# Summing a token's two expert rows with a 128-row product and two column tiles

## The chip, the cores and the metric

The kernel runs on one core of a Trainium2 chip. The metric is the device time of one execution in microseconds; lower is better. A core has TensorE (matrix products, into PSUM), VectorE, ScalarE and GpSimd (elementwise work), SyncE (SP, which here issues most transfers), and 16 transfer engines that all queues share.

## The reference, cut to what matters

One inference step of a small decoder with two layers, for 1024 prompt tokens and 8 sample tokens of 1024 float32 features. Each layer mixes (sliding-window attention and a short gated convolution), normalises, and then runs a mixture of 32 experts, of which each token uses two:

```python
x = layer_norm(ALPHA * x + mixer(x), ln1_g, ln1_b)
x = layer_norm(ALPHA * x + hier_moe(x), ln2_g, ln2_b)   # hier_moe: y[token] = sum over its 2 experts of gate * mlp_e(x[token])
```

The change is in how the two expert results of a token are added and handed to that last layer norm.

## The kernel before, in words

**Data.** Tokens lie in nine tiles: tiles 0 to 7 have 128 tokens (NB = 8), tile 8 (t == NB) has the 8 sample tokens. T is 1032. The DRAM tensor `ytok` has the shape (2, T, 1024): for each token and each of its two experts (k = 0, 1) one row of 4 KB, written by indirect transfers of the experts' results (the residual is already in them). `rows_of` is the same tensor seen as 2T rows, so row t*128 + i holds token i of tile t for k = 0, and row T + t*128 + i holds it for k = 1.

**The seam and the tail.** After the 32 experts of a layer, SP waits for all indirect writes and then loads the rows (L515 to L532). `first_in(t)` brings the k = 0 rows of tile t into `xin[t]`, and `second_in(t)` the k = 1 rows into `second[t]`. A transfer has 128 partitions and 512 KB; both count up the semaphore `l2_in{t}`. In the last layer this is done for all nine tiles. In the first layer it is done for tiles 0 to 4 (SUMMED = 5); tiles 5 to 8 only get their first row from SP, in between, and GpSimd later adds the second row to it with an accumulating transfer (`second_added`, L2067 to L2072). GpSimd issues that after its part of the norm of tile t - 5 and after waiting for `l2_in{t}`.

**The sum on TensorE.** `outputs_summed(l, t)` (L556 to L571) waits for both rows of a tile, and for a free pair of PSUM banks (a ring of two pairs in the first layer, of four in the last). For each half of the 1024 features it makes two products with the identity as weights, which accumulate in one bank: the first rows, then the second rows (L567, L569). A float32 product appears as two instructions in the trace. In the first layer tiles 0 and 1 are summed at the end of the layer (L1077); the sums of tiles 2, 3 and 4 stand in the next layer's program, each ahead of `x_turned(t)`, the transposes of tiles 0, 1 and 2 (L599 to L602). Then the projections of the next layer begin (`first_project`, L595) with the turns of tiles 3 to 8 between them.

**The norm.** VectorE takes statistics of the sum in PSUM (`statistics2`, L1862), GpSimd the inverse root (`inverse2`), VectorE subtracts the mean and multiplies by the gain into `xin[t]` (`shifted2`, L1881), then multiplies by the inverse root and adds the bias (`scaled2`, L1887), and counts up `x2_ready`. In the first layer the order is shifted(p-1), statistics(p), scaled(p-1). In the last layer ScalarE takes the statistics of tiles 1 to 8 (L1286, L1298). SP stores each finished tile from `xin[t]` (L536), after all the loads in its queue. The next layer's transposes read `xin[t]`.

**A load elsewhere.** At the start of each layer SP loads the output weights `wo` in three transfers, with rows of 4 KB: two of 1 MB into partitions 0 to 63 and 64 to 127, then one of 2 MB into all partitions:

```python
                for h in range(NKV):
                    sp.dma_start(wo[h * HD:(h + 1) * HD, 0:4],
                                 a["w_o"][l, h * QPK * HD:(h + 1) * QPK * HD].rearrange("(k p) n -> p k n", p=HD)
                                 ).then_inc(s["wo_in"], 16)
                sp.dma_start(wo[:, 4:8], a["w_o"][l, NH * HD:].rearrange("(k p) n -> p k n", p=P)).then_inc(s["wo_in"], 16)
```

**Column tiles elsewhere.** The down projection of an expert with at most 64 tokens uses two column tiles of TensorE, one product into PSUM partitions 0 to 63 (L969) and one into 64 to 127 (L971).

Of the kernel before, what the change touches and what calls it, by code (L numbers as in the profile page):

```python
# [11 lines left out]
ALU = mybir.AluOpType  # L12
# [3 lines left out]
P = 128  # L16
DM = 1024
KD = DM // P
DEPTH = 2
SEQ = 1024  # L20
NS = 8
T = SEQ + NS
NB = SEQ // P
# [19 lines left out]
HALF = P // 2  # L43
# [10 lines left out]
BASE = 2  # L54
# [3 lines left out]
SUMMED = 5  # L58


def rows_in(l, t):

    return 16 + (32 if t < SUMMED else 16) * l


def settle(eng, passed):


    eng.sem_inc(passed, 1)
# [35 lines left out]
def build(nc, a):  # L105

    ctx = ExitStack()
    with ctx:
        def sb(name, shape, dt=F32):
            return ctx.enter_context(nc.sbuf_tensor(name, shape, dt))  # L110
# [7 lines left out]
        rows_of = a["ytok"].rearrange("k t d -> (k t) d")  # L118


        ident = sb("ident", [P, P])
        ones = sb("ones", [P, P])
        upper = sb("upper", [P, P])
        iota = sb("iota", [P, P])
        masks = sb("masks", [P, 3, 2 * P])
# [46 lines left out]
        def at(off, *shape, parts=P):  # L172
            n = int(np.prod(shape))
            v = arena[0:parts, off:off + n]
            if len(shape) == 2:
                return v.rearrange("p (a b) -> p a b", a=shape[0])
            if len(shape) == 4:
                return v.rearrange("p (a b c d) -> p a b c d", a=shape[0], b=shape[1], c=shape[2])
            if len(shape) == 3:
                return v.rearrange("p (a b c) -> p a b c", a=shape[0], b=shape[1])  # L180
            return v
# [23 lines left out]
        def ws(off, *shape, parts=P):  # L205
# [59 lines left out]

        passed_over = at(0, 2, DM)
        xin = [at(29552 + 1024 * t, DM) for t in range(NB)] + [at(27496, DM, parts=NS)]
        second = [at(14448 + 1024 * t, DM) for t in range(4)] + [at(o, DM) for o in (37744, 38768, 39792, 28528)] \
            + [at(26464, DM, parts=NS)]
        FIRST3 = [(c, ch) for ch in range(NCH) for c in range(3)]  # L270
        ROTATED = FIRST3 + [(c, ch) for c in (3, 4) for ch in range(NCH)]
        TURNED_WITH = {(1, 0): 3, (2, 0): 4, (0, 1): 5, (1, 1): 6, (2, 1): 7, (0, 2): 8}
# [1 line left out]
        ps = ctx.enter_context(nc.psum_tensor("ps", [P, 8, 512], F32))  # L274
# [52 lines left out]
        def _(sp):  # L327
# [13 lines left out]
            def tile_rows(t):  # L341
                return P if t < NB else NS
# [22 lines left out]
            for l in range(DEPTH):  # L365
# [149 lines left out]
                def first_in(t):  # L515
                    sp.dma_start(xin[t][0:tile_rows(t)], rows_of[t * P:t * P + tile_rows(t), :]
                                 ).then_inc(s[f"l2_in{t}"], 16)

                def second_in(t):
                    sp.dma_start(second[t][0:tile_rows(t)], rows_of[T + t * P:T + t * P + tile_rows(t), :]  # L520
                                 ).then_inc(s[f"l2_in{t}"], 16)

                if l < DEPTH - 1:
                    for t in range(SUMMED):
                        first_in(t)
                        second_in(t)
                        if 0 < t < SUMMED:
                            first_in(SUMMED + t - 1)
                else:
                    for t in range(NT):  # L530
                        first_in(t)
                        second_in(t)  # L532
                for t in range(NT):
                    sp.wait_ge(s["x2_ready"], BASE + NT * (l + 1) + t + 1)
                    settle(sp, s["sp_passed"])
# [8 lines left out]
        def _(pe):  # L544
            raise_to_base(pe, "tensor")
            mm = nc.tensor.matmul
# [9 lines left out]

            def outputs_summed(l, t):

                rows = P if t < NB else NS
                ring = 4 if l == DEPTH - 1 else 2  # L560
                pe.wait_ge(s[f"l2_in{t}"], BASE + rows_in(l, t) + 32)
                if t >= ring:
                    pe.wait_ge(s["l2_used"], BASE + NT * l + t - ring + 1)
                settle(pe, s["pe_passed"])
                for h in range(2):
                    cols = slice(h * 512, (h + 1) * 512)
                    mm(ps[0:rows, 2 * (t % ring) + h, :], ident[0:rows, 0:rows], xin[t][0:rows, cols],  # L567
                       start=True, stop=False)
                    last = mm(ps[0:rows, 2 * (t % ring) + h, :], ident[0:rows, 0:rows], second[t][0:rows, cols],  # L569
                              start=False, stop=True)  # L570
                last.then_inc(s["l2_mm"], 1)  # L571

            for l in range(DEPTH):
# [465 lines left out]
                with pe.If(pe.value_load(over[0:1, OVER:OVER + 1], min_val=0, max_val=OVER) > 0):  # L1039
                    pe.wait_ge(s["ov_m"], BASE + l + 1)  # L1040
                    settle(pe, s["pe_passed"])
                    for i in range(2 * NT):
                        last = mm(ps[:, 0, 0:2 * OVER], over_slot[:, i], over_block[:, i].rearrange("p q n -> p (q n)"),
                                  start=(i == 0), stop=(i == 2 * NT - 1))
# [5 lines left out]
                    with pe.Fori(0, OVER) as o:  # L1050
                        n = OVER * l + o
                        pe.wait_ge(s["ov_xin"], BASE + n + 1)
                        for k in range(KD):
                            last = tr(ps[:, k // 4, (k % 4) * P:(k % 4 + 1) * P], xg_by_row[0][:, k], ident[:])
# [3 lines left out]
                        for f in range(FD):  # L1058
                            for w, bank in ((wg, 2), (wu, 4)):
                                for k in range(KD):  # L1060
                                    last = mm(ps[:, bank, f * P:(f + 1) * P], w[2].rearrange("p k (c f) -> p k f c", f=FD)[:, k, f],
                                              xgT[:, 0, k], start=(k == 0), stop=(k == KD - 1))
                        last.then_inc(s["ov_gu"], 1)
                        pe.wait_ge(s["ov_h"], BASE + n + 1)
                        for h in range(2):
                            for f in range(FD):
                                last = mm(ps[:, 6 + h, :], hT[:, f], wd[0][:, f, h * 512:(h + 1) * 512],
                                          start=(f == 0), stop=(f == FD - 1))
# [244 lines left out]
        def _(dve):  # L1313
            raise_to_base(dve, "vector")
            v = nc.vector
            step = Steps(dve, s["dve_step"])
# [12 lines left out]
            for k in range(2):  # L1329
                step.mark(v.tensor_scalar(token[:, k, 1:NT], tokens1[:, 0:NB], float(k * T - 1 - NONE), None, ALU.add))  # L1330
                step.mark(v.tensor_scalar(token[:, k, 0:1], tokens1[:, NB:NT], float(k * T - 1 - NONE), None, ALU.add))
            step.mark(v.tensor_scalar(bias_row[:], rank_desc[:], NE - FIRST + 0.5, 1e6, ALU.is_gt, ALU.mult))
            for h in range(2):
                step.mark(v.tensor_tensor(perm[:, h * NE:(h + 1) * NE], ident[0:64, h * NE:(h + 1) * NE],
# [20 lines left out]
            for l in range(DEPTH):  # L1355

                for i, (r, ch) in enumerate(ROTATED):
                    cols = slice(ch * CH, (ch + 1) * CH)
                    dve.wait_ge(s["act_ev"], BASE + l * NTILE * NCH + i + 1 + 6)
                    for q in range(4):  # L1360
                        to, of = slice(32 * q, 32 * q + 32), slice(32 * (q ^ 1), 32 * (q ^ 1) + 32)
                        last = v.scalar_tensor_tensor(rot[to, i % 2], ztmp[of, r % 3, cols], 2.0 * (q % 2) - 1,  # L1362
                                                      sinT[of, cols], ALU.mult, ALU.mult)
# [489 lines left out]
                def on_tensor(t):  # L1853
                    return l == DEPTH - 1 or t < SUMMED
# [7 lines left out]
                def statistics2(t, r, p):  # L1862
                    if on_tensor(t):
                        dve.wait_ge(s["l2_mm"], BASE + SUMMED * l + t + 1)
                    else:
                        dve.wait_ge(s[f"l2_both{t}"], 16 * (l + 1))
                    dve.wait_ge(s["l2_stat"], BASE + NT * l + p)
                    for h in range(2):
                        step.mark(v.bn_stats(stat[r, 6 * h:6 * h + 6], summed(t, r)[:, h * 512:(h + 1) * 512]))
                    step.wait()  # L1870
                    settle(dve, s["dve_passed"])
                    v.bn_aggr(mv[r, p % 2], stat[r]).then_inc(s["l2_stat"], 1)

                def shifted2(t, r, p):
                    if l < DEPTH - 1 or p == 0:
                        dve.wait_ge(s["l2_stat"], BASE + NT * l + p + 1)
                        shift, by = mv[r, p % 2, 0:1], ALU.subtract
                    else:
                        dve.wait_ge(s["l2_square"], BASE + p)
                        shift, by = sums[r, p % 4, 1:2], ALU.add  # L1880
                    v.scalar_tensor_tensor(xin[t][r], summed(t, r), shift, lnp[r, 2], by, ALU.mult  # L1881
                                           ).then_inc(s["l2_used"], 1)

                def scaled2(t, r, p):
                    dve.wait_ge(s["l2_used"], BASE + NT * l + p + 1)
                    dve.wait_ge(s["l2_rstd"], BASE + NT * l + p + 1)
                    v.scalar_tensor_tensor(xin[t][r], xin[t][r], rstd[r, p % 2, 0:1], lnp[r, 3], ALU.mult, ALU.add  # L1887
                                           ).then_inc(s["x2_ready"], 1)

                rows_at = [slice(0, P if t < NB else NS) for t in range(NT)]  # L1890
                statistics2(0, rows_at[0], 0)
                if l < DEPTH - 1:
                    for p in range(1, NT):
                        shifted2(p - 1, rows_at[p - 1], p - 1)
                        statistics2(p, rows_at[p], p)
                        scaled2(p - 1, rows_at[p - 1], p - 1)
                    shifted2(NT - 1, rows_at[NT - 1], NT - 1)
                    scaled2(NT - 1, rows_at[NT - 1], NT - 1)
                else:
                    shifted2(0, rows_at[0], 0)  # L1900
                    for p in range(1, NT):
                        shifted2(p, rows_at[p], p)
                        scaled2(p - 1, rows_at[p - 1], p - 1)
                    scaled2(NT - 1, rows_at[NT - 1], NT - 1)
# [264 lines left out]
```

## Time and profile before

| | |
|---|---|
| time, median of 3 runs | 2174.56 us (2174.32 to 2181.47) |
| the profiled execution's own time | 2183.16 us |
| its span | 2181.3 us |
| TensorE matmul busy | 2072.5 us, 95% of the span |
| VectorE, ScalarE, GpSimd busy | 805.1, 325.7, 222.1 us |
| mean granted TensorE clock | 0.974 of full speed |
| transfers | 535.92 MB, mean 246 GB/s |

Times in views of the trace are microseconds from the span's start; those of the two stretches of interest are about 1056 to 1085 (the seam between the layers) and 2129 to 2181 (the tail). A row of the chain of waits gives the start and the length of one link. A row of the timeline gives the start, the length, the engine, the line and the operation; PE is TensorE's products, SPq are issues on SP's queue.

### The profile page before, as it was taken

The page shows a single profiled execution, that of the slowest core. Times are in us where ns is not written, and L with a number is a line of the kernel's source. Part 1 is how long each engine was busy: PE and PEld are TensorE (multiplying, and loading weights), DVE is VectorE, ACT ScalarE, POOL GpSimd, SP SyncE. Part 2 cuts the span into 40 slices and gives each one's busy share as a digit, 9 for nine tenths or more (in the row PEclk, how much of TensorE's full clock was granted, in tenths as well). Part 3 has the DMA queues.
Part 4 walks back from the last instruction along what each step waited for, and adds up shares of the span by engine and source line. Part 5 has one row for each costly group of instructions (what it writes and reads, how often), then busy time and mean ns, then how long its engine had stood idle before and what let it go on. Part 6 is the DMA issues. An engine that isn't in the chain of part 4 may idle for free.

```text
span 2181.3 us, 32300 instructions
## 1 busy us (share of the span) xinstructions
PE 2072.5 (95%) x13024; PEld 1221.7 (56%) x13024; DVE 805.1 (37%) x1547; ACT 325.7 (15%) x856; POOL 222.1 (10%) x250
## 2 busy tenths in 40 slices
PE   8999999989999999899799999999999999999986
PEld 5666655565555655455366666555645556554542
DVE  4512166672222222222482123766622221222224
ACT  2011123311111011111010111333001110110103
POOL 1200000000111111110231000000001100111101
PEclk9999999999999999999899999999999999999997
DMA  6601131348999999998634101413689999999956
GB/s 223 193 30 38 41 128 68 113 158 316 360 392 400 414 384 396 392 387 334 231 123 120 39 29 32 158 59 116 228 325 391 399 406 395 392 388 394 379 219 236
DMA packets 77465, 535.92 MB, mean 246 GB/s; under 512 B 14586, under 2 KB 23674, under 8 KB 52386
## 3 DMA queue, kind: packets, MB, share of 16 engines
q1 hardware_dynamic: 64050, 498.37, 59.5%
q0 software_dynamic: 13264, 35.44, 4.8%
q8 instruction: 107, 1.75, 0.3%
q14 instruction: 44, 0.36, 0.0%
HBM read 494.14 MB, written 54.08 MB: 251 GB/s over the span
## 4 chain that ended last, share of the span: by engine, by line
PE 91%; DVE 4%; issue 3%; DMA 1%; ACT 1%; POOL 1%; DVEq 0%; SPq 0%; POOLq 0%
PE ps L925 20%; PE ps L616 19%; PE ps L969 10%; PE ps L763 9%; PE ps L905 6%; PE ps L595 4%; PE ps L893 3%; PE ps L976 3%; PE ps L921 3%; PE ps L949 2%; PE ps L567 1%; PE ps L963 1%; PE ps L569 1%; PE ps L805 1%; PE ps L705 1%
## 5 line engine op out<-in xcount | busy, mean ns | idle before, releaser
L927 PE MATMUL ps<-arena 128*64 128x256 f32 x1920 | 450.9, 391 | 0.0
L925 PE MATMUL ps<-arena 128*64 128x256 f32 x1920 | 450.9, 391 | 0.0
L616 PE MATMUL ps<-arena 128*128 128x344 f32 x1440 | 421.2, 453 | 0.0
L925 PEld LDWEIGHTS ps<-arena 128*64 128x64 f32 x1920 | 255.0, 135 | 175.9 <-issue 23.9
L616 PEld LDWEIGHTS ps<-arena 128*128 128x128 f32 x1440 | 272.0, 190 | 142.9 <-issue 3.6
L969 PE MATMUL ps<-arena 128*64 128x512 f32 x480 | 236.5, 639 | 22.3 <-issue 19.9
L927 PEld LDWEIGHTS ps<-arena 128*64 128x64 f32 x1920 | 254.5, 135 | 0.0
L971 PE MATMUL ps<-arena 128*64 128x512 f32 x480 | 236.8, 640 | 0.0
L763 PE MATMUL ps<-arena 128*128 128x512 f32 x448 | 195.9, 594 | 2.7 <-issue 2.7
L1703 DVE SCALAR_TENSOR_TENSOR arena<-ps,gates,arena 64x256 f32<-64x256 f32 (+1 forms) x128 | 60.9, 476 | 354.9 <-ACT arena L1228 354.9
L1970 POOL DMA_INDIRECT ytok<-arena,gidx x64 | 60.3, 942 | 955.3 <-DVE arena L1731 924.2
L763 PEld LDWEIGHTS ps<-arena 128*128 128x128 f32 x448 | 84.0, 190 | 105.1 <-issue 105.1
L969 PEld LDWEIGHTS ps<-arena 128*64 128x64 f32 x480 | 65.1, 145 | 137.0 <-issue 133.8
L1228 ACT ACTIVATE arena<-ps 64x256 f32<-64x256 f32 (+1 forms) x128 | 48.9, 382 | 618.9 <-PE ps L927 535.7
L905 PE MATMUL ps<-arena 128*32 128x256 f32 x2048 | 129.4, 405 | 10.7 <-DVE arena L1724 9.2
L905 PEld LDWEIGHTS ps<-arena 128*32 128x32 f32 x2048 | 68.2, 112 | 77.4 <-issue 36.2
L1093 ACT COPY arena<-ps 128x344 f32<-128x344 f32 x90 | 40.1, 446 | 361.1 <-PE ps L616 324.1
L1944 POOL TENSOR_SCALAR rstd<-mv 128x1 f32<-128x1 f32 (+1 forms) x18 | 21.6, 1203 | 693.8 <-DVE mv L1353 693.8
L595 PE MATMUL ps<-arena 128*128 128x344 f32 x288 | 86.0, 454 | 5.6 <-ACT arena L1100 5.6
L1362 DVE SCALAR_TENSOR_TENSOR arena<-arena,sinT 32x344 f32<-32x344 f32 x120 | 76.6, 638 | 26.2 <-ACT arena L1093 16.5
L1119 ACT ACTIVATE arena<-arena,sm 128x256 f32<-128x256 f32 x128 | 63.7, 499 | 90.5 <-DVEq L1438 90.5
L595 PEld LDWEIGHTS ps<-arena 128*128 128x128 f32 x288 | 53.6, 190 | 32.3 <-issue 6.5
(262 smaller groups left out, 2133.0 us busy)
## 6 DMA issues: line engine op xcount, KB each, us to landing
arena<-in_w_gate SPq DMA_DIRECT2D x64, 2048.0 KB, 24.0
arena<-in_w_up SPq DMA_DIRECT2D x64, 2048.0 KB
arena<-in_w_down SPq DMA_DIRECT2D x64, 2048.0 KB
arena<-in_w_in SPq DMA_DIRECT2D x36, 512.0 KB, 3.5
ytok<-arena SPq DMA_DIRECT2D x32, 512.0 KB, 3.5
arena<-ytok SPq DMA_DIRECT2D x29, 512.0 KB, 9.3
arena<-out_y_all SPq DMA_DIRECT2D x16, 512.0 KB, 3.5
out_y_all<-arena SPq DMA_DIRECT2D x16, 512.0 KB
```

The lines of the kernel that those rows point to most:

```text
L595: last = mm(ps[:, bank, 0:CH], wring[:, c, k * P:(k + 1) * P], xT[:, k, ch * CH:(ch + 1) * CH], start=(k == 0), stop=(k == KD - 1))
L616: last = mm(ps[:, 3 * half + ch, 0:CH], wring[:, slot, k * P:(k + 1) * P], xT[:, k, ch * CH:(ch + 1) * CH], start=(k == 0), stop=(k == KD ...
L763: last = mm(ps[0:rows, 6 + n, :], mix[k], wo[:, k, n * 512:(n + 1) * 512], start=(k == 0), stop=(k == KD - 1))
L893: last = tr(ps[:, k // 4, (k % 4) * P:(k % 4) * P + rows], xg_by_row[slot + 2 * (turn % 2)][0:rows, k], ident[0:rows, 0:rows])
L905: last = mm(ps[QUART * t:QUART * (t + 1), 5, 0:256], xgT[:, slot, k, HALF:MID], w[slot3][q][:, k], start=(k == 0), stop=(k == KD - 1))
L921: last = mm(ps[:, 2 + q, at_c:at_c + 256], xgT[:, slot, k], w[slot3][q][:, k], start=(k == 0), stop=(k == KD - 1))
L925: mm(ps[HALF:P, 2 + q, 0:256], xgT[:, slot, k, 0:HALF], wg_half[slot3][q][:, k], start=(k == 0), stop=(k == KD - 1))
L927: last = mm(ps[0:HALF, 2 + q, 0:256], xgT[:, slot, k, 0:HALF], wu_half[slot3][q][:, k], start=(k == 0), stop=(k == KD - 1))
L969: mm(ps[0:HALF, 6, :], hT[:, f, 0:HALF], wd[slot][:, f, 0:512], start=(f == 0), stop=(f == FD - 1))
L971: last = mm(ps[HALF:P, 7, :], hT[:, f, 0:HALF], wd[slot][:, f, 512:DM], start=(f == 0), stop=(f == FD - 1))
L976: last = mm(ps[QUART * t:QUART * (t + 1), 5, 0:256], hT[:, f, HALF:MID], wd[slot][:, f, t * 256:(t + 1) * 256], start=(f == 0), stop=(f == ...
L1362: last = v.scalar_tensor_tensor(rot[to, i % 2], ztmp[of, r % 3, cols], 2.0 * (q % 2) - 1, sinT[of, cols], ALU.mult, ALU.mult)
```

## The change

The two rows of a token are put on partitions i and 64 + i of one tile: `xin[t]` gets both rows of the first 64 tokens of tile t, `second[t]` both rows of the other 64. `both` is a 128 x 64 matrix of two identities, so one product with it as weights adds the two rows of 64 tokens. Its result goes to PSUM partitions 0 to 63 for `xin[t]` and 64 to 127 for `second[t]`, which are two column tiles of TensorE. Each tile is loaded by four transfers of 64 partitions and 256 KB in place of two of 128 partitions and 512 KB. The 8-row tile gets 16 partitions, `both_s`, and its own weights, `both8`. VectorE builds both matrices at the start. In the first layer, VectorE now scales tile 0 before it takes the statistics of tile 1. The tiles that GpSimd adds (5 to 8 in the first layer) stay as they were.

```diff
 def rows_in(l, t):
-    return 16 + (32 if t < SUMMED else 16) * l
+    return 16 + (64 if t < SUMMED else 16) * l
...
+        both = sb("both", [P, HALF])
+        both8 = sb("both8", [2 * NS, NS])
...
-        second = [at(14448 + 1024 * t, DM) for t in range(4)] + [at(o, DM) for o in (37744, 38768, 39792, 28528)] \
-            + [at(26464, DM, parts=NS)]
+        second = [at(14448 + 1024 * t, DM) for t in range(4)] + [at(o, DM) for o in (37744, 38768, 39792, 28528)]
+        both_s = at(27496, DM, parts=2 * NS)
...
-                def second_in(t):
-                    sp.dma_start(second[t][0:tile_rows(t)], rows_of[T + t * P:T + t * P + tile_rows(t), :]
-                                 ).then_inc(s[f"l2_in{t}"], 16)
+                def both_in(t):
+                    if t == NB:
+                        for k in range(2):
+                            sp.dma_start(both_s[k * NS:(k + 1) * NS], a["ytok"][k, SEQ:T, :]
+                                         ).then_inc(s[f"l2_in{t}"], 16)
+                        return
+                    for tile, r0 in ((xin[t], t * P), (second[t], t * P + HALF)):
+                        for k in range(2):
+                            sp.dma_start(tile[k * HALF:(k + 1) * HALF], a["ytok"][k, r0:r0 + HALF, :]
+                                         ).then_inc(s[f"l2_in{t}"], 16)
 
                 if l < DEPTH - 1:
                     for t in range(SUMMED):
-                        first_in(t)
-                        second_in(t)
+                        both_in(t)
                         if 0 < t < SUMMED:
                             first_in(SUMMED + t - 1)
                 else:
                     for t in range(NT):
-                        first_in(t)
-                        second_in(t)
+                        both_in(t)
...
             def outputs_summed(l, t):
-                rows = P if t < NB else NS
                 ring = 4 if l == DEPTH - 1 else 2
-                pe.wait_ge(s[f"l2_in{t}"], BASE + rows_in(l, t) + 32)
+                pe.wait_ge(s[f"l2_in{t}"], BASE + rows_in(l, t) + (64 if t < NB else 32))
...
                 for h in range(2):
-                    cols = slice(h * 512, (h + 1) * 512)
-                    mm(ps[0:rows, 2 * (t % ring) + h, :], ident[0:rows, 0:rows], xin[t][0:rows, cols],
-                       start=True, stop=False)
-                    last = mm(ps[0:rows, 2 * (t % ring) + h, :], ident[0:rows, 0:rows], second[t][0:rows, cols],
-                              start=False, stop=True)
+                    bank, cols = 2 * (t % ring) + h, slice(h * 512, (h + 1) * 512)
+                    if t == NB:
+                        last = mm(ps[0:NS, bank, :], both8[:], both_s[:, cols], start=True, stop=True)
+                    else:
+                        mm(ps[0:HALF, bank, :], both[:], xin[t][:, cols], start=True, stop=True)
+                        last = mm(ps[HALF:P, bank, :], both[:], second[t][:, cols], start=True, stop=True)
                 last.then_inc(s["l2_mm"], 1)
...
+            step.mark(v.tensor_tensor(both[:], ident[:, 0:HALF], ident[:, HALF:P], ALU.add))
+            step.mark(v.tensor_tensor(both8[:], ident[0:2 * NS, 0:NS], ident[0:2 * NS, NS:2 * NS], ALU.add))
...
                     for p in range(1, NT):
                         shifted2(p - 1, rows_at[p - 1], p - 1)
+                        if p == 1:
+                            scaled2(0, rows_at[0], 0)
                         statistics2(p, rows_at[p], p)
-                        scaled2(p - 1, rows_at[p - 1], p - 1)
+                        if p > 1:
+                            scaled2(p - 1, rows_at[p - 1], p - 1)
```

## Rows read from the trace of the kernel before

**Rows 1.** The page: busy time and share of each engine.
```profile
PE 2072.5 (95%) x13024; PEld 1221.7 (56%) x13024; DVE 805.1 (37%) x1547; ACT 325.7 (15%) x856; POOL 222.1 (10%) x250
```

**Rows 2.** The chain of waits over the seam: start, length, link.
```profile
1056.37 4.57 DMA arena<-ytok
...
1063.12 1.71 PE ps L569 x2
...
1083.20 0.89 PE ps L583 x8
...
1085.27 4.87 PE ps L595 x16
```

**Rows 3.** The chain of waits over the tail.
```profile
2129.57 4.43 DMA arena<-ytok
2134.14 2.04 PE ps L567 x2
...
2163.22 0.86 PE ps L569 x2
...
2166.74 0.87 PE ps L569 x2
```

**Rows 4.** Timeline of the last expert of each layer: products in column tiles.
```profile
1045.54 1.06 PE L969 MATMUL ps<-arena 128*64 128x512 f32 x1
...
1045.57 1.06 PE L971 MATMUL ps<-arena 128*64 128x512 f32 x1
...
1046.39 1.06 PE L969 MATMUL ps<-arena 128*64 128x512 f32 x1
...
2122.08 0.59 PE L969 MATMUL ps<-arena 128*64 128x512 f32 x1
...
2122.51 0.59 PE L969 MATMUL ps<-arena 128*64 128x512 f32 x1
```

**Rows 5.** Timeline of the seam: issues on SP's and GpSimd's queues.
```profile
1056.37 0.43 SPq L520 DMA_DIRECT2D arena<-ytok  x1
1056.84 0.43 SPq L516 DMA_DIRECT2D arena<-ytok  x1
...
1070.52 1.02 POOL L2071 DMA_DIRECT2D arena<-ytok  x1
```

**Rows 6.** Windows of seam and tail; last columns: granted clock, transfer engines' share, GB/s.
```profile
1059.00:1073.00 14.00, 11.92 (x21) 5.18 (x22) 4.55 (x8) 0.00 (x0) 1.90 (x4) 0.72 1.03 411
...
1065.00:1067.00 2.00, 2.00 (x3) 0.67 (x2) 0.00 (x0) 0.00 (x0) 0.00 (x0) 0.54 1.04 422
...
1075.00:1085.00 10.00, 9.07 (x36) 4.84 (x34) 9.30 (x15) 2.91 (x3) 5.71 (x7) 1.00 1.04 260
...
2132.00:2150.00 18.00, 15.86 (x32) 7.03 (x33) 3.60 (x5) 3.63 (x8) 1.25 (x4) 0.82 1.02 408
```

**Rows 7.** Windows of the `wo` load in both layers; same columns.
```profile
77.00:79.00 2.00, 2.00 (x9) 1.31 (x8) 1.97 (x3) 0.00 (x0) 1.23 (x1) 1.00 1.02 201
79.00:81.00 2.00, 2.00 (x9) 1.31 (x8) 1.15 (x3) 0.00 (x0) 0.00 (x0) 1.00 1.04 223
...
75.00:85.00 10.00, 10.00 (x36) 6.53 (x36) 6.88 (x12) 0.89 (x2) 2.47 (x2) 1.00 1.02 206
...
1148.00:1158.00 10.00, 10.00 (x36) 6.55 (x35) 6.52 (x11) 1.34 (x3) 2.60 (x3) 1.00 1.02 204
87.00:91.00 4.00, 4.00 (x15) 2.64 (x14) 2.56 (x5) 0.45 (x1) 0.61 (x2) 1.00 1.01 401
```

**Rows 8.** Timeline of the tail: ScalarE's and VectorE's work on one tile.
```profile
2160.68 1.03 ACT L1286 ACTIVATE arena<-ps 128x1024 f32<-128x1024 f32 x1 [1.13 <-PE ps L569]
...
2161.69 1.11 ACT L1298 ACTIVATE arena<-ps,sums 128x1024 f32<-128x1024 f32 x1
...
2162.93 1.28 DVE L1881 SCALAR_TENSOR_TENSOR arena<-ps,sums,lnp 128x1024 f32<-128x1024 f32 x1 [0.96 <-ACT arena L1298]
...
2164.12 1.28 DVE L1887 SCALAR_TENSOR_TENSOR arena<-arena,rstd,lnp 128x1024 f32<-128x1024 f32 x1
```

## The prediction

> **What bounds the kernel now.** I read the busy shares first. TensorE holds 95% of the span [rows 1], so a change counts where TensorE stands still or where it does the changed work itself. The change touches two short stretches only: the seam between the two layers and the tail of the second layer. So I next read the chain of waits over each of them. At the seam it goes through the load of a tile's two rows, then the sums of tiles 0 to 4 on TensorE with the transposes of the next layer between them, then a copy on ScalarE, and the first projection begins at 1085.27 [rows 2]. In the tail it goes through the same load, then 36 products in one unbroken row until 2167.6 (2166.74 and 0.87 more) [rows 3]; ScalarE, VectorE and the last store follow, 13.7 us up to the end of the span at 2181.3. At both places a load ends first and TensorE then sets the pace, so two prices decide: how fast the rows arrive, and how long a tile's sum holds TensorE.
>
> **TensorE's part.** Before, a tile takes four products, each of two instructions (the chain's rows "x2"), with the full 128-column weights. Two instructions take 1.71 us just after a wait, at the low clock (1.2 GHz) [rows 2], and 0.86 us at the high one (2.4 GHz) [rows 3]. That is 6.8 or 3.43 us for a tile. After, a tile takes four products with 64-column weights, two and two in different column tiles. The down projection does this already: an instruction of L969 and one of L971 start 0.03 us apart, and the next L969 starts 0.86 us later at the low clock and 0.43 us later at the high one [rows 4]. A pair thus costs what one full-width instruction costs, and a tile's sum falls to 3.43 us (low) or 1.71 us (high). The last tile, of 8 rows, goes from four products to two that stand alone: 1.71 us at the high clock, 3.43 at the low one. If nothing else changed, this would take 1.71 us from each of eight tiles of the tail.
>
> **The loads' part.** The bytes stay the same (1.05 MB for a tile), but each transfer is 64 partitions wide instead of 128. Five tiles at the seam go from 10 transfers to 20, eight tiles of the tail from 16 to 32. Issuing one costs SP about 0.45 us (two starts are 0.47 apart [rows 5]), so the first tile's last transfer is issued 0.9 us later; after that issuing, 1.8 us for a tile, is faster than either rate below. The question is the rate. With 128 partitions the loads run at 411 GB/s at the seam and at 408 in the tail, with the transfer engines' share at 1.0 [rows 6]: 2.56 us for a tile. The trace has one load of the new kind: w_o goes into partitions 0-63 and 64-127 in two transfers of 1 MB, one right after the other, from rows of 4 KB. It moves 206 GB/s in layer 0 and 204 in layer 1, with the engines' share again at 1.0, and the following transfer into all 128 partitions is back at 401 [rows 7]. Two queued transfers to opposite halves did not make up for each other. At 205 GB/s a tile takes 5.1 us. The new transfers change halves every 256 KB and not once per MB. The 2 us in which w_o changes halves show 223 GB/s beside 201 before it [rows 7], about 0.04 MB or 0.2 us gained at a hand-over; four in each tile would bring 5.1 down to 4.3 us, and none leaves 5.1. As in layer 1 windows vary as much with no hand-over in them, I lean to the upper end and take 4.9 us.
>
> The Trainium skill, SBUF — State Buffer, section "Can I just issue two DMAs to hit both halves?", says no: a 64-partition transfer reaches half of the memory's ports, and two concurrent ones, at partition 0 and at 64, were only 6% faster than one. The w_o rows agree. By its 6% a tile would take 4.8 us in place of 5.1.
>
> **The seam.** Before, tile 0's rows are there at 1060.94 (1056.37 and 4.57) and the last of the five sums ends at 1083.2, where the turn of tile 2 begins [rows 2]. After, in the order of the queue, with 4.9 us for a tile and 1.28 us for each first row of tiles 5 to 7 that lies between: tile 0 at 1063.3 (2.34 later than at 2.56 us), tile 1 at 1068.2, then tiles 2, 3 and 4 each 1.28 and 4.9 later. The adding transfers of GpSimd fall among them. The first was issued at 1070.52 [rows 5]; its three full ones and the first stores leave 260 GB/s in the ten microseconds from 1075 [rows 6], in which 2.6 MB would take 6.3 us at 411: 3.7 us lost, 1.2 for each of three, and 1.3 for its own half megabyte. Before they ran behind the loads. Now each can run before one of the loads of tiles 2 to 4, as it waits for a first row that lies one tile ahead of them: 2.5 us each. Tile 4 is then there at 1068.2 + 3 x (1.28 + 2.5 + 4.9) = 1094.3. Its sum takes 1.7 or 3.4 us, since TensorE stands idle for a few microseconds before each tile; I take the middle, 2.6. It ends at 1096.9, 13.7 us later than before. The turn and copy behind it keep their length. The clock came back about 5 us after the first product: at the seam it is still 0.54 between 1065 and 1067, and the mean of 0.82 over the 18 us from 2132 means 6.5 us at 0.5, up to 2138.5 [rows 6]; a projection that starts low would lose half of that, 2.5 us, and I count 1.2. The seam costs +14.9 us (ends: +2.4 with 4.3 us, no collision and the high clock; +17 to +21 with 5.1 us, dearer adding transfers and the low clock). The projections behind it are TensorE's own work, so this isn't won back.
>
> VectorE scales tile 0 one step earlier, ahead of tile 1's statistics. This frees tile 0 some 2 us sooner, but its turn on TensorE stands behind the sum of tile 2, which now waits for rows: nothing. If rows came at the old rate it would be worth up to 1 us. Its two small operations that build the summing weights lie in the first layer's preparation, a few tenths of a microsecond on an engine that is 37% busy [rows 1]: nothing, and 0.3 us without that cover. Nothing new waits on GpSimd's or SP's queue but what the later rows delay: the stores of the finished tiles lie behind all loads, as before.
>
> **The tail.** Before, tile 0's rows are there at 2134.0 [rows 3]. After, at 2136.3, and tile 7's 7 x 4.9 later, at 2170.6. From then TensorE has that tile and the 8-row one to do, 2.6 us each by the same middle: 2175.8, against 2167.6 before. +8.2 us (ends: +1.9 with 4.3 us and the high clock, +12 with 5.1 and the low one). The stores have about 2.6 MB to catch up once the loads are out, 6.4 us at 408 GB/s, which ends inside the 13.7 us that follow.
>
> **Sum.** 14.9 + 8.2 = 23.1 us. The profiled execution took 2183.2 us (span 2181.3), 8.6 above the median of 2174.56; the sum made against it gives 2206.3, and on the median 2197.7. I say 2197.5.
>
> **The rivals.** (1) The loads keep their rate, because small transfers to the two halves run side by side. For it: w_o has only one change of halves in a layer, so no row shows an alternating load. Against it: 204 to 206 GB/s with both transfers in the queue. Then the tail is paced by the loads (2.56 us a tile), by ScalarE (1.03 and 1.11 us and their read-outs) and VectorE (1.28 and 1.28) [rows 8], all about 2.6 us in place of TensorE's 3.43. The first sum ends at 2134.9 + 3.4, and the 8-row tile's near 2159.2, 8.4 us earlier; the seam gives 2.3 us by the first sum and some 0.7 by the shorter later ones. -11.4 us: 2163. It decides if a tile arrives in under about 3.2 us. (2) They overlap in part, 300 GB/s, 3.5 us a tile: the tail's pace is then the old 3.43 and its end is set by two short sums, -4 us; the seam gains on VectorE's side and loses by the collisions, +2 to +6. About 2174, no change. (3) The column tiles don't overlap and a sum keeps 3.43 us: rows 4 speak against it, and under a 4.9 us load it would add under 4 us; it stands inside the upper end.
>
> **How the numbers follow.** Half rate, as reckoned: 0.74; its own range is 2179 (+4 by the lower ends) to 2208. Full rate 0.14, partly overlapped 0.12. The predicted time is that of the first. The range is 2170 to 2208: it takes in the second rival and leaves out the first (0.14) and what lies above the upper ends (0.05). A measurement here tells about 0.5%, 11 us, from no change. Slower by more: 0.70 of the first case and 0.02 of the partial one, 0.72. Within: 0.04 of the first, 0.10 of the partial, 0.06 of full rate, 0.20. Faster: 0.08.
>
> **What would show it.** In the windows of the changed kernel's loads: 205 to 240 GB/s with a share of 1.0, where 408 to 411 stood; if it is 400, the forecast falls. TensorE waiting on the load before each tile, not only before tile 0. Pairs of sum instructions 0.43 or 0.86 us apart. The first projection 13 to 16 us later after tile 0's load is issued than now; if only some 7, the adding transfers didn't collide. The last sum 6 to 12 us later in the tail. The prediction is wrong if a tile takes under 4 us to arrive.

## The result, and the profile after

The changed kernel takes 2198.17 us (median of 7 runs, 2194.13 to 2209.7) against 2179.57 of the kernel before on the same chips (2174.32 to 2189.01). The ratio is 1.009, 95% interval [1.0071, 1.011]: slower by 0.9%. The medians differ by 18.6 us and the ratio makes 20 us (15 to 24 by its interval). The forecast was 2197.5 us and slower.

The page after, the same row as [rows 1]:

```profile
span 2207.8 us, 32320 instructions
...
PE 2065.4 (94%) x13020; PEld 1213.1 (55%) x13020; DVE 804.9 (36%) x1549; ACT 324.9 (15%) x856; POOL 221.5 (10%) x250
```

TensorE has 7 us less to do and the span is 26.5 us longer. The windows of the changed kernel, same columns as [rows 6], the first three at the seam and the last three in the tail:

```profile
1063.00:1065.00 2.00, 0.00 (x0) 0.00 (x0) 0.00 (x0) 0.00 (x0) 0.00 (x0) 0.50 0.99 231
...
1091.00:1093.00 2.00, 0.68 (x4) 0.40 (x6) 1.13 (x1) 0.00 (x0) 0.89 (x3) 1.00 0.99 381
...
1097.00:1099.00 2.00, 0.89 (x3) 0.68 (x4) 2.00 (x2) 0.97 (x1) 1.62 (x2) 1.00 0.32 107
...
2153.00:2183.00 30.00, 19.12 (x48) 4.61 (x48) 10.22 (x10) 8.94 (x19) 3.03 (x8) 0.63 1.03 229
...
2187.00:2189.00 2.00, 1.16 (x6) 0.54 (x8) 1.49 (x2) 0.56 (x3) 0.74 (x2) 0.94 1.03 418
2189.00:2191.00 2.00, 2.00 (x5) 0.10 (x2) 0.98 (x1) 0.32 (x1) 0.00 (x0) 0.50 1.03 420
```

For thirty microseconds of the tail the transfer engines are as fully occupied as before (share 1.03) and move 229 GB/s where [rows 6] have 408. From 2187 on, when the last row has come and the stores of 128 partitions run, the rate is 418 to 420. The timeline of TensorE shows what this does. First the seam, tiles 0 to 4, then the first projection:

```profile
1065.82 1.08 PE L576 MATMUL ps<-arena,both 128*64 128x512 f32 x1 [13.07 <-DMA arena<-ytok]
...
1070.44 0.61 PE L576 MATMUL ps<-arena,both 128*64 128x512 f32 x1 [1.02 <-DMA arena<-ytok]
...
1076.40 1.09 PE L576 MATMUL ps<-arena,both 128*64 128x512 f32 x1 [4.02 <-DMA arena<-ytok]
...
1084.39 1.09 PE L576 MATMUL ps<-arena,both 128*64 128x512 f32 x1 [3.54 <-DMA arena<-ytok]
...
1092.32 0.61 PE L576 MATMUL ps<-arena,both 128*64 128x512 f32 x1 [2.43 <-DMA arena<-ytok]
...
1098.11 4.87 PE L602 MATMUL ps<-arena 128*128 128x344 f32 x16 [1.19 <-ACT arena L1107]
```

TensorE now waits for the load before each tile, where before it waited once. The steps are 4.6 and 6.0 us, then 8.0 and 7.9. In the tail the eight tiles come 4.6 us apart; the first, the last, and the 8-row tile:

```profile
2155.48 1.09 PE L576 MATMUL ps<-arena,both 128*64 128x512 f32 x1 [12.95 <-DMA arena<-ytok]
...
2187.84 0.64 PE L576 MATMUL ps<-arena,both 128*64 128x512 f32 x1 [2.62 <-DMA arena<-ytok]
...
2190.57 3.58 PE L574 MATMUL ps<-arena,both 16*8 16x512 f32 x4
```

To compare kernels I take two lengths from each trace. The seam is from the issue of its first load to the start of the first projection; the tail is from the issue of its first load to the end of the last sum. Before, they are 29.3 us (1055.99 to 1085.27) and 38.4 us (2129.18 to 2167.6). After, they are 39.8 us (1058.33 to 1098.11) and 46.0 us (2148.18 to 2194.15). That is +10.5 and +7.6, in all +18.1 us, beside the 18.6 us between the medians. The other 8 us of the profiled executions' difference lie outside them, 2.3 ahead of the seam and 6.2 from the projection to the tail, where the change touches nothing. The latter stretch is 1043.9 us long before, 1050.1 after, and between 1039.1 and 1048.0 in the eight experiments below, without relation to what they change. The two lengths vary too where nothing on their path was changed, by 1 to 1.5 us: e7 has a seam 1.0 us shorter than before and a tail 1.5 us longer. A difference of one microsecond between two of these lengths shows nothing by itself.

### The profile page after: what moved, and what is told of

Same layout as the page of the kernel before. It is cut to its first block, busy times and chain, and to the rows that moved or that the text cites. A ratio compares the mean times of both kernels' runs of the same rounds, so it can differ in the third digit from the quotient of the medians.

```text
span 2207.8 us, 32320 instructions
## 1 busy us (share of the span) xinstructions
PE 2065.4 (94%) x13020; PEld 1213.1 (55%) x13020; DVE 804.9 (36%) x1549; ACT 324.9 (15%) x856; POOL 221.5 (10%) x250
## 4 chain that ended last, share of the span: by engine, by line
PE 88%; DVE 4%; issue 3%; DMA 2%; SPq 1%; ACT 1%; POOL 1%; DVEq 0%; POOLq 0%
PE ps L932 20%; PE ps L623 19%; PE ps L976 10%; PE ps L770 9%; PE ps L912 6%; PE ps L602 4%; PE ps L900 3%; PE ps L983 3%; PE ps L928 3%; DMA arena<-ytok 2%; PE ps L956 2%; SPq L529 1%; PE ps L970 1%; PE ps L812 1%; PE ps L712 1%
## 5 line engine op out<-in xcount | busy, mean ns | idle before, releaser
L623 PEld LDWEIGHTS ps<-arena 128*128 128x128 f32 x1440 | 272.0, 190 | 142.9 <-issue 3.6
L770 PEld LDWEIGHTS ps<-arena 128*128 128x128 f32 x448 | 84.0, 190 | 105.1 <-issue 105.1
L1371 DVE SCALAR_TENSOR_TENSOR arena<-arena,sinT 32x344 f32<-32x344 f32 x120 | 74.9, 624 | 26.2 <-ACT arena L1100 16.5
L576 PE MATMUL ps<-arena,both 128*64 128x512 f32 x52 | 39.0, 894 | 48.3 <-DMA arena<-ytok 48.3
```

Source lines behind the costliest of these rows:

```text
L623: last = mm(ps[:, 3 * half + ch, 0:CH], wring[:, slot, k * P:(k + 1) * P], xT[:, k, ch * CH:(ch + 1) * CH], start=(k == 0), stop=(k == KD ...
L770: last = mm(ps[0:rows, 6 + n, :], mix[k], wo[:, k, n * 512:(n + 1) * 512], start=(k == 0), stop=(k == KD - 1))
```

## The experiments

The theory (H) is that of the prediction: a load into one half of the partitions runs at a little over half the rate, and the two halves do not make up for each other in a queue. The rivals: the loss comes from the number and size of the transfers (S), from the column tiles, or from the source that jumps between the two sets of rows.

**e1_half_loads**, the loads' part alone, on the kernel before:

```diff
...
+                def both_in(t):
+                    if t == NB:
+                        first_in(t)
+                        second_in(t)
+                        return
+                    for tile, r0 in ((xin[t], t * P), (second[t], T + t * P)):
+                        for h in range(2):
+                            sp.dma_start(tile[h * HALF:(h + 1) * HALF], rows_of[r0 + h * HALF:r0 + (h + 1) * HALF, :]
+                                         ).then_inc(s[f"l2_in{t}"], 16)
...
```

> The loads' part of the change alone: the kernel before, with every 128-partition row load of tiles on TensorE split into two of 64 partitions; sums with the identity as before. If loads into one half of the partitions are slow (theory H), the tail's tiles arrive 4.6 us apart as in the changed kernel, the sums hide under them but for the last two, and the kernel is as slow as the changed one or some 3 us slower: +18 to +24 us. If the loss came from the column tiles or their weights (rival), this kernel runs as before, within 3 us.

Measured: ratio 1.0102 [1.0083, 1.0121], 22 us slower. The window of its tail:

```profile
2153.00:2180.00 27.00, 23.86 (x48) 9.41 (x47) 10.22 (x10) 8.98 (x19) 3.02 (x8) 0.91 1.04 229
```

The rate is that of the changed kernel, 229 GB/s, with sums of full width and a source that does not jump. The seam takes 41.9 us and the tail 46.9: +12.6 and +8.4. The changed sums and the source are thus not what costs the time; beside this kernel, the changed one is 3 us shorter in the two stretches.

**e2_pairs**, the same sums, with a token's two rows on partitions 2i and 2i+1:

```diff
...
-                        for k in range(2):
-                            sp.dma_start(tile[k * HALF:(k + 1) * HALF], a["ytok"][k, r0:r0 + HALF, :]
-                                         ).then_inc(s[f"l2_in{t}"], 16)
+                        sp.dma_start(tile, a["ytok"][:, r0:r0 + HALF, :].rearrange("k t d -> t k d")
+                                     ).then_inc(s[f"l2_in{t}"], 16)
...
-            step.mark(v.tensor_tensor(both[:], ident[:, 0:HALF], ident[:, HALF:P], ALU.add))
+            step.mark(v.tensor_tensor(both[:], ident[:].rearrange("p (m k) -> p k m", k=2)[:, 0],
+                                      ident[:].rearrange("p (m k) -> p k m", k=2)[:, 1], ALU.add))
...
```

> The same sums in column tiles, but the two rows of a token lie on partitions 2i and 2i+1, so that 64 tokens come in one 128-partition transfer of 512 KB; the summing weights are paired accordingly. If only the reach of a transfer over the partitions matters (H), loads run near 400 GB/s, tiles 2.6 us apart, and the time is about 11 us under the kernel before (ratio 0.995). If a source that jumps between the two row sets is itself slow (rival), windows show 230 GB/s and the time is that of the changed kernel, +18 us.

Measured: 2172.74 us, ratio 0.997 [0.9958, 0.9983], faster by 0.3%, some 6.5 us and not 11. Its window over the tail's loads, and two tiles in a row of its timeline:

```profile
2133.00:2153.00 20.00, 15.14 (x56) 4.36 (x56) 10.10 (x10) 10.25 (x22) 3.02 (x8) 0.84 1.01 397
```

```profile
2148.99 0.61 PE L574 MATMUL ps<-arena,both 128*64 128x512 f32 x1 [0.62 <-DMA arena<-ytok]
...
2151.55 0.61 PE L574 MATMUL ps<-arena,both 128*64 128x512 f32 x1 [0.62 <-DMA arena<-ytok]
```

397 GB/s and 2.56 us a tile, so a source that jumps between the two sets of rows isn't slow. The tail takes 28.6 us, 9.8 less than before. The seam takes 32.3 us, 3.0 more than before, where I expected some 3 less. Its own wait says why:

```profile
1080.27 1.08 PE L574 MATMUL ps<-arena,both 128*64 128x512 f32 x1 [5.84 <-DMA arena<-ytok]
```

This is tile 4, 20.6 us after tile 0 (1059.66). Four tiles at 2.56 us and three first rows at 1.28 make 14.1, and before the change its rows came 14.5 us after those of tile 0. As tile 0 is normalised sooner, GpSimd issues its first adding transfer 12.0 us after the first load's issue (1066.24), where it was 14.5 before [rows 5], and two more about 4 us apart (1070.38, 1074.08). The issue times and the view's times from issue to landing put the landings of the first two at 1075.3 and 1079.2, ahead of tile 4's rows (1080.1); before the change tile 4's rows had landed (1075.4) ahead of the first (1078.3). So the faster sums start transfers that then hold up the load on the path; e6 tests it.

**e3_grouped**, the changed kernel with the order lower, lower, upper, upper:

```diff
-                    for tile, r0 in ((xin[t], t * P), (second[t], t * P + HALF)):
-                        for k in range(2):
+                    for k in range(2):
+                        for tile, r0 in ((xin[t], t * P), (second[t], t * P + HALF)):
```

> The changed kernel with the four transfers of a tile in the order lower, lower, upper, upper half in place of lower, upper, lower, upper: half as many changes of half. By the hand-over theory (the engines that finish early go on in the other half, 0.2 us gained at each change) the tail's rate falls from 229 GB/s to about 217 and tiles arrive 4.85 us apart, +4 us in the two stretches. If the rate has nothing to do with the changes of half, it stays at 229 GB/s and 4.57 us.

Measured: ratio 1.0092 [1.0068, 1.0116], which cannot be told from the changed kernel. The window of its tail:

```profile
2150.00:2182.00 32.00, 19.49 (x54) 5.11 (x56) 12.70 (x12) 10.53 (x23) 3.76 (x10) 0.71 1.04 217
```

217 GB/s and a mean of 4.87 us a tile, as the hand-over theory wanted: with halves changing every 1 MB 205, every 512 KB 217, every 256 KB 229. The 4 us did not come. The slower loads lengthen the seam by 1.5 us, but the tail is 0.6 us shorter, as the clock happened to be high at its last two sums: its 8-row tile takes 1.88 us where the changed kernel's row above has 3.58.

**e4_mid64**, tail loads of the same number and size into partitions 32 to 95; two of each four go to unused places, so the last layer's sums are of stale data:

```diff
...
+                    for t in range(NB):
+                        for k, tile in enumerate((xin[t], free[2 * t], second[t], free[2 * t + 1])):
+                            r0 = t * P + HALF * (k // 2)
+                            sp.dma_start(tile[QUART:P - QUART], a["ytok"][k % 2, r0:r0 + HALF, :]
+                                         ).then_inc(s[f"l2_in{t}"], 16)
...
```

> The changed kernel whose tail loads go, in the same number and size (four of 64 partitions and 256 KB for a tile), into partitions 32 to 95, which lie across both halves; two of four go to unused places, so the last layer's sums are of stale data and its outputs are not the reference's. If the half matters (H), the tail's windows show about 400 GB/s and tiles arrive 2.6 to 2.8 us apart. If the number of transfers or their size matters (rival S: 32 issues of 0.64 us, 256 KB each), the rate stays near 229 GB/s and 4.57 us.

```profile
2137.00:2153.00 16.00, 13.68 (x48) 4.28 (x48) 7.31 (x8) 7.78 (x16) 2.28 (x6) 0.79 1.01 393
```

393 GB/s, 2.56 us a tile, a tail of 29.3 us. Number and size are the same, only the place differs: S falls. (One execution, read for its windows alone.)

**e5_firsts_last**, the changed kernel with the first rows of tiles 5 to 8 behind all rows of tiles 0 to 4:

```diff
                         both_in(t)
-                        if 0 < t < SUMMED:
-                            first_in(SUMMED + t - 1)
+                    for t in range(SUMMED, NT):
+                        first_in(t)
```

> The changed kernel, but at the seam the first rows of tiles 5 to 8 are loaded after all rows of tiles 0 to 4, so no adding transfer of GpSimd can run among them. If the collisions cost what the changed kernel's trace suggests (tiles 3 and 4 arrive 8.0 us after the one before, of which 4.6 are their own, 1.3 the first row between and 2.1 an adding transfer), all tiles arrive 4.6 us apart, tile 4 about 8 us earlier, and the seam from the first load's issue to the first projection shrinks from 39.8 to 32 us or a little more. If the adding transfers run in gaps (rival), only the moved first rows count, 3.8 us.

Measured: ratio 1.0086 [1.0057, 1.0115]; the seam takes 37.4 us and not 32. Tiles 1 and 2 come 4.6 us apart and TensorE waits for no later load, so the collisions are gone. The landings say what they cost. The following are the last two issues for tile 4 and their time to landing, of which the maximum is that of the last, first in this kernel, then in the changed one:

```profile
L529 SPq DMA_DIRECT2D arena<-ytok x2: 597/597/597, 1065.9 to 1066.6; - x2
...
DMA to landing us min/median/max: 12.6/12.9/13.1
```

```profile
L529 SPq DMA_DIRECT2D arena<-ytok x2: 596/596/597, 1071.2 to 1071.8; - x2
...
DMA to landing us min/median/max: 20.0/20.2/20.4
```

Tile 4's rows land at 1079.6 here, 18.4 us after those of tile 0 (1061.3), and at 1092.2 in the changed kernel, 26.5 us after tile 0's (1065.7). The difference is 8.1 us, as the expectation had it. The three first rows account for 3.8 of it (3 x 1.28); the other 4.3 us are adding transfers, and the rival (3.8 us in all) falls.

The seam did not gain these 8 us, as another wait has come in their place. Two rows of its timeline:

```profile
1081.49 1.02 POOL L2083 DMA_DIRECT2D arena<-ytok  x1 [13.68 <-DMA arena<-ytok]
...
1083.66 1.28 DVE L1896 SCALAR_TENSOR_TENSOR arena<-arena,rstd,lnp 128x1024 f32<-128x1024 f32 x1 [8.44 <-POOL rstd L2077]
```

GpSimd does its work here in the order of the program. It waits 13.68 us for the first row of tile 5, and the inverse root of tile 1, for which VectorE waits 8.44 us, stands behind that wait. Neither my theory nor the rival had this.

**e6_pairs_late**, the pairs kernel with the first rows of tiles 5 to 7 one tile later:

```diff
...
                         both_in(t)
-                        if 0 < t < SUMMED:
-                            first_in(SUMMED + t - 1)
+                        if t > 1:
+                            first_in(SUMMED + t - 2)
+                    first_in(NT - 1)
```

> The kernel with pairs on partitions 2i and 2i+1, and the first rows of tiles 5 to 7 each one tile later in SP's queue. There tile 4 came only 20.6 us after tile 0, held up by first rows and adding transfers, and the seam took 32.3 us against 29.3 before the change. With fewer of them ahead, tile 4 should come by some 16 us after tile 0 and the seam take 27 to 29 us; the tail stays at 28.6 us from the first issue to the last sum. Expected 3 to 5 us under the pairs kernel, ratio 0.995. If VectorE or the sample tile sets the seam's end instead, it stays at 0.997.

Measured: 2167.85 us, ratio 0.9945 [0.9928, 0.9962], some 12 us faster than the kernel before; it is the best version found. Against the pairs kernel it gains some 5 us, but the two intervals just overlap. Tile 4 and the first projection:

```profile
1076.60 1.08 PE L575 MATMUL ps<-arena,both 128*64 128x512 f32 x1 [1.74 <-DMA arena<-ytok]
...
1082.13 4.87 PE L601 MATMUL ps<-arena 128*128 128x344 f32 x16 [1.19 <-ACT arena L1106]
```

Tile 4 comes 16.5 us after tile 0 and no longer 20.6, with one first row fewer (1.3 us) ahead of it. The first adding transfer is issued 13.3 us after the first load (1068.32) and lands at 1077.6, after tile 4's rows (1076.5), where in the pairs kernel two had landed before them. This bears out the reading of e2. The seam takes 27.1 us and the tail 28.5: -2.1 and -9.9 us.

**e7_order_only**, VectorE's new order alone on the kernel before (the last part of the change's diff).

> The kernel before with VectorE's new order alone (tile 0 scaled ahead of tile 1's statistics). Theory: nothing, within 1 us, as the turn of tile 0 stands behind the sum of tile 2 on TensorE. Rival: a turn that comes earlier brings the projections up to 2 us forward.

Measured: ratio 0.9999 [0.9983, 1.0015]: nothing, as expected. The seam takes 28.3 us, 1.0 less than before, but the new order is not the reason. The first product of tile 0, that of tile 1 and the turn of tile 0, first before the change, then here:

```profile
1061.08 2.05 PE L567 MATMUL ps<-arena,ident 128*128 128x512 f32 x2 [10.66 <-DMA arena<-ytok]
...
1067.45 1.02 PE L567 MATMUL ps<-arena,ident 128*128 128x512 f32 x2
...
1074.32 1.04 PE L583 MATMUL ps<-ident,arena 128*128 128x128 f32 x8
```

```profile
1059.80 2.05 PE L567 MATMUL ps<-arena,ident 128*128 128x512 f32 x2 [10.59 <-DMA arena<-ytok]
...
1065.42 1.02 PE L567 MATMUL ps<-arena,ident 128*128 128x512 f32 x2
...
1072.29 1.04 PE L583 MATMUL ps<-ident,arena 128*128 128x128 f32 x8
```

In both the turn follows the sum of tile 2 with no wait, 6.87 us after tile 1's first product. The time is gained ahead of that, in the sum of tile 0 (5.6 us in place of 6.4), because the granted clock rose sooner: it is 0.74 from 3.2 to 5.2 us after the first product (1063 to 1065), where before the change it is 0.54 from 3.9 to 5.9 us [rows 6]. VectorE had not begun by then, so the new order can't be the cause. The rival, up to 2 us, falls too.

**e8_two_queues**, the changed kernel's tail loads, lower halves from SP's queue, upper halves from ScalarE's:

```diff
...
+                    for t in range(NB):
+                        for tile, r0 in ((xin[t], t * P), (second[t], t * P + HALF)):
+                            nc.scalar.dma_start(tile[HALF:P], a["ytok"][1, r0:r0 + HALF, :]
+                                                ).then_inc(s[f"l2_in{t}"], 16)
```

> The changed kernel whose tail loads are issued from two queues: the lower halves from SP, the upper halves from ScalarE's queue at the same time, same transfers otherwise. If an engine takes both queues in turn and the halves really are separate resources, both are filled at once and tiles arrive 2.6 us apart (about 400 GB/s). If the engines stay in step, each writing to one half at a time, the rate stays between 205 and 240 GB/s and tiles 4.4 to 5.1 us apart.

Two of its windows:

```profile
2138.00:2140.00 2.00, 0.00 (x0) 0.00 (x0) 0.00 (x0) 0.00 (x0) 0.00 (x0) 0.50 1.04 227
...
2150.00:2152.00 2.00, 1.89 (x8) 0.49 (x8) 0.00 (x0) 0.49 (x4) 0.00 (x0) 1.00 1.03 322
```

It was run once (2185.7 us). It starts at 227 GB/s and settles at 322, 3.24 us a tile, and the tail takes 34.6 us. Both expectations missed: two queues fill the halves better than one, but not fully. Why it takes 6 us to get there stays open.

## Why the prediction was right

**The rate of the loads** was the step that decided, and it held; e1 shows that it alone makes the loss, e4 that the place of the 64 partitions makes the rate. 4.9 us were taken for a tile between 4.3 and 5.1; it is 4.6 in both stretches (one step of the tail's seven is 5.0). The gain at a hand-over, which I mostly discounted as noise in the windows, is real: e3's 217 GB/s was forecast from it. What the Trainium skill states in SBUF — State Buffer, section "Can I just issue two DMAs to hit both halves?", that two concurrent transfers to the two halves were only 6% faster than one, was borne out in its direction for one queue. Its 6% stands beside the 12% that 229 makes over 205 with transfers of 256 KB, and 6% is what 217 makes with 512 KB in a row; no run has a 64-partition load entirely alone. With the loads from two queues e8 reached 322 GB/s, more than the section's plain "no" allows, and here the measurement decides.

**TensorE's part** held: pairs of instructions stand 0.86 or 0.43 us apart, as in [rows 4]. In the pairs kernel, whose loads keep their rate, it shows what it is worth: 9.8 us in the tail, by the pace the first rival gave (2.6 us a tile, forecast -8.4).

**The seam** was forecast at +14.9 and measured +10.5. That is less than the 13 to 16 us that the prediction named as its sign and more than the 7 of no collision. Tile 0's sum starts 2.4 us later after the first issue than before (forecast 2.34). From there to tile 4 the forecast had 31.0 us and the trace has 26.5. Shorter tiles make 1.2 of that. The rest is the term that was mis-sized, the adding transfers: I let three run before tile 4's load, at 2.5 us each, and two did, at 2.1 to 2.2 us each. Two landed ahead of tile 4's rows (1092.2), at 1083.3 and 1088.1, and the third only at 1097.6; their price is what the steps leave (8.0 less 4.6 less 1.3) and half of the 4.3 us of e5. The clock term was misplaced: I gave 1.2 us to the projection, which starts at 1.00 and takes the same 4.87 us as before [rows 2]; in its place the turn ahead of it runs low (1.65 us where the chain before has 0.89).

**The tail** was forecast at +8.2 and measured +7.6, of two errors that nearly cancel: tile 7's sum starts 39.7 us after the first issue (forecast 41.4), and the two sums behind take 6.3 us (forecast 5.2), mostly at the low clock.

**VectorE's new order** was put at nothing, and e7 shows nothing. What it would be worth where the rows come at full rate and the sums are short, as in the pairs kernel, was not measured.

**The total** is nearer than its terms, by luck. The two stretches make 18.1 us against the 23.1 forecast, so the working is 5 us too high, and the forecast of 2197.5 still comes within 1 us of the median of 2198.17 because the kernel before ran 5 us slower in the second set of runs, 2179.57.

**The first rival** is refuted as it stands: loads of 64 partitions don't keep the rate. What it says of kernels whose loads do keep it can be held against the pairs kernels, and there it was right about TensorE and wrong about the seam. Even at the full rate the seam got 3 us longer (e2), because the adding transfers moved in front of tile 4; with the queue reordered (e6) both stretches gain and the total is -12 us, about what the rival had named (-11.4).

## What to carry to other kernels

Look at which partitions a transfer covers, not only at its bytes: two loads of 64 partitions are not one of 128, and alternating between the halves in one queue wins back little. If a layout needs two rows of a source side by side in one product, interleave them over the partitions so that one transfer still covers all 128. And when a step gets faster, look at what it sets off: here GpSimd's transfers then came ahead of a load on the critical path, and moving loads back made an in-order engine wait with work behind it.

## What the runs showed of the hardware that was not expected

- 64 partitions are not slow in themselves: partitions 32 to 95 run at 393 GB/s (e4), partitions 0 to 63 and 64 to 127 in turn at 229.
- The alternating rate depends on the length of a turn: 205, 217 and 229 GB/s at 1 MB, 512 KB and 256 KB. Two queues, one for each half, reach 322.
- An issue on SP's queue took 0.43 us at the seam of the kernel before [rows 5] and 0.59 to 0.60 in the changed one, for the first rows too, whose transfer is unchanged (L518):

```profile
1069.44 0.58 SPq L518 DMA_DIRECT2D arena<-ytok  x1
1070.07 2.36 SPq L529 DMA_DIRECT2D arena<-ytok  x4
```

  It was hidden here, as four issues (2.6 us) are shorter than a tile's transfer. In e5, where the four first rows are issued one after another behind all other loads, they took 0.37 to 0.59 us, with a median of 0.43. What it comes from is open.
